# Layer trunk on one core: unread products between the halves of the input, rounding among square sums, a store from the scalar engine, and changed places for rotation, retention scores and routing

## The chip, the core and the metric

One program on one core of a Trainium2 chip. The time is device microseconds of one execution; several executions are taken and the median is compared. TensorE multiplies, VectorE and ScalarE work elementwise, GpSimd issues a few transfers, SyncE (SP) issues nearly all loads and the stores. A profile is one execution recorded by the hardware profiler.

## The reference

A decoder trunk of two layers on 256 tokens of width 1024, in float32:

```
layer 0: RMSNorm -> one projection (3744 columns) -> MLA (8 heads) beside retention (8 heads)
         -> output projection -> residual; RMSNorm -> SwiGLU (3584) -> residual
layer 1: RMSNorm -> one projection -> sliding-window attention (16 heads) beside stick-breaking (8)
         -> output projection -> residual; RMSNorm -> top-2-of-8 expert SwiGLU -> residual
final RMSNorm
```

Retention rotates its queries and keys, takes scores per head, multiplies them by a decay and by the values. The router takes `logits = h @ router` (8 columns), the two largest per token, and a softmax over these.

## The kernel before, in words

The program is one block with a written-out instruction list per engine; engines meet only through semaphores, and each engine's list is its order of work. Every weight is split: ScalarE rounds a piece of 128 x 1024 (a "unit") to a short float (`l0_hi`, `hi_unit`, L327), VectorE subtracts to get the rest (`l0_lo`, `lo_unit`, L331), and TensorE makes three products of the halves (`mm3`, L318 to L320). Four units are in flight; unit d + 3 is split while unit d is multiplied.

*Start.* SP loads a few constants, then x in two halves of 512 columns, with pieces of the first projection between them, then the other tables, `w_ukv`, `w_uq`, the router, and from unit 8 on pieces of the projection into four slots that have come free. TensorE multiplies a block of ones three times (`fill`, L2586), transposes the first half of x (`norm_pe`, L376), waits for the second, transposes it and goes on to the units 0 to 3 (the kv latents and the rotary key), 4 to 7 (the query latents), 8 to 15 (retention queries and keys) and so on (`l0_pe`, `project`). ScalarE takes the square sums of x (`sums_of_squares`, L340), VectorE their inverse root.

*Latents.* After unit 4 TensorE transposes the kv latents (`turn_latent`, L805), VectorE copies them with a gain (`latent_turned(3, 2, 0)`, L590) at d = 5 of its loop, ahead of the rest of unit 8, and TensorE multiplies them by `w_ukv` after units 6 and 7 (`keys_values`, L815). `rope_key` (L599 to L606) follows the rest of unit 9.

*Units 16 to 31.* TensorE alternates units with the eight heads of MLA: `scores`, `turn` (L862), `values`. VectorE does `minimum`, `normalised` (L649 to L652) and the rotation `rope_ret` of retention, whose second part stands whole at d = 17 and d = 18. Rotated blocks are transposed by `turn_ret` (L846) at the units in `RT_AT`, retention scores (`ret_scores`, L880, L881) are taken at the units in `RET_AT`, VectorE multiplies them by the decay (`decayed`).

*Routing.* After the last output product of layer 1, TensorE transposes the right half of h (L2183), multiplies by the router (L2175, 8 columns a product), makes unread products (L2190) while VectorE ranks the logits, gets places by products with a triangle and ones (L2200 to L2204), gathers the rows of the first expert by products with a pick matrix (`first_pe`, L2222, L2223), and transposes them (L2228) when VectorE has scaled them (L2351). ScalarE rounds (L2286), VectorE takes the rest (L2356), and the first expert's gate product begins (L318, `pre_hi`).

*End.* The four quarters of the output are stored by SP (L2528) in the order (0, 0), (0, 1), (1, 1), (1, 0), each when VectorE or ScalarE has scaled it.

The order on VectorE that the text speaks of:

```python
                if d == 5:
                    dve.wait_ge(tables_in, 16)
                    latent_turned(3, 2, 0)
...
                if d + 3 < L0_UNITS:
                    l0_lo(dve, d + 3)
```

Of the kernel before, what the change touches and what calls it, by code (L numbers as in the profile page):

```python
# [13 lines left out]
P = 128  # L14
# [65 lines left out]
def trunk(nc, x, consts, decay_t, ab_w_in, w_uq, w_ukv, ab_w_out, f_gate, f_up, f_down,  # L80
          cd_w_in, cd_w_out, router, m_gate, m_up, m_down, moe_gain, final_gain, out):
    with ExitStack() as ctx:
# [119 lines left out]

        PRE_HI_AT = (CONST_OFF + 4 * (CONST_AT["cos_m"] + 40), ARENA, ARENA + 4096, XN_AT)
# [21 lines left out]
        def sem(name):  # L225
# [53 lines left out]
                             "rstd_banked", "rstd_set"))  # L279
        first_banked, first_scaled, first_turned, first_hi, first_lo = (  # L280
# [86 lines left out]

        def norm_pe(pe, use, ks=range(KD)):
            for k in ks:
                if use == 0 and k % 4 == 0:  # L370
                    pe.wait_ge(x_in[k // 4], 16)
                    pe.wait_ge(consts_in, 16)
                if use and k % 4 == 0:
                    pe.wait_ge(h_done, 4 * use - 2 + k // 2)
                for tb in range(TB):
                    ins = nc.tensor.transpose(norm_bank(use, k)[:, tb * P:tb * P + P],  # L376
                                              h[:, tb, k * P:k * P + P], const("ident"))
                if k % 2:
                    ins.then_inc(xT_banked, 1)
# [72 lines left out]
        def l0_act(act):  # L452
# [86 lines left out]
            for d in range(L0_UNITS):  # L539
# [18 lines left out]
                if d + 3 < L0_UNITS and d != 1:  # L558
                    l0_hi(act, d + 3)
# [3 lines left out]
                if d == 1:  # L563
                    sums_of_squares(act, 0, False, (1,))
# [19 lines left out]
        def l0_dve(dve):  # L584
# [40 lines left out]
            def rope_ret(part, tb):  # L625
                dve.wait_ge(ab_evac, part + 3)
                w = slice(512 * part, 512 * part + 512)
                t = rope_t.rearrange("p (a h d) -> p a h d", a=2, d=64)
                rope(rqk_raw[:, tb, w].rearrange("p (h d) -> p h d", d=64),
                     bc(const("cos_r", 64 * tb, 64 * tb + 64), 8), bc(const("sin_r", 64 * tb, 64 * tb + 64), 8), 32,  # L630
                     t[:, 0], t[:, 1], rqk[:, tb, w].rearrange("p (h d) -> p h d", d=64)).then_inc(rqk_done, 1)
                dve.wait_ge(rqk_done, 2 * part + tb + 1)

# [73 lines left out]
            for d in range(L0_UNITS):  # L707
# [25 lines left out]
                if d in (17, 18):  # L733
                    rope_ret(1, d - 17)
# [20 lines left out]
        def l0_pe(pe):  # L755
# [150 lines left out]
            for d in range(L0_UNITS):  # L906
# [6 lines left out]
                if d == 4:  # L913
                    turn_latent(lat_kv, 2, (4,), 0)
# [1246 lines left out]
        lg, gt, eq, gt_eq, rank = (rt[:, a:b] for a, b in ((36, 52), (64, 192), (192, 320), (64, 320), (320, 336)))  # L2161
        sel = sel_r.bitcast(F32)
# [4 lines left out]
        def route_pe(pe):  # L2167
            def logits(ks):
                for k in ks:
                    if k < 6:  # L2170
                        pe.wait_ge(xT_hi_done, 3 * KD + k + 1)
                    else:
                        pe.wait_ge(x32_act, k - 5)
                    for tb in range(TB):
                        ins = nc.tensor.matmul(pb[4][:, tb * NE:tb * NE + NE], xT32[:, xT32_at[k], tb * P:tb * P + P],  # L2175
                                               router_sb[:, k, :], start=(k, tb) == (0, 0), stop=k == KD - 1,
                                               skip_group_check=True)
                return ins
# [13 lines left out]
            pe.wait_ge(router_in, 16)  # L2192
# [18 lines left out]
        def first_pe(pe):  # L2211

            pe.wait_ge(pick_done, 2)
            pe.wait_ge(rstd_done, 4)
            for tb in range(TB):
                ins = nc.tensor.matmul(pb[0][:, 0:1], pick[:, tb, :], rstd[:, tb:tb + 1], start=tb == 0, stop=tb == 1)
# [8 lines left out]
            for k in range(KD):  # L2225
                if k % 4 == 0:
                    pe.wait_ge(first_scaled, k // 4 + 1)
# [18 lines left out]
        def route_act(act):  # L2246
# [59 lines left out]
        def route_dve(dve):  # L2306
# [10 lines left out]
            rest(1, 0)  # L2317
            dve.wait_ge(logits_banked, 1)
            vs(nc.vector.tensor_copy(lg, pb[4][:, 0:16]))
# [13 lines left out]
            inverse_rms(dve, 3)  # L2333
            rest(1, 1)

# [7 lines left out]
            early_lo(dve, 0)  # L2343
# [4 lines left out]
            for r in range(2):  # L2348
                w = slice(512 * r, 512 * r + 512)
                dve.wait_ge(first_banked, r + 1)  # L2350
                nc.vector.scalar_tensor_tensor(out=first_rows[:, w], in0=pb[6 + r], scalar=place_rstd,  # L2351
                                               in1=g_moe_row[:, w], op0=ALU.mult, op1=ALU.mult).then_inc(first_scaled, 1)
            for j in range(4):
# [3 lines left out]
                                        first_bank(j), f32(hi_),  # L2357
                                        ALU.subtract).then_inc(first_lo, 1)
            vs(nc.vector.tensor_reduce(cmax, pb[5][:, 16:24], AX, ALU.max))
# [31 lines left out]
        def last_root(act, part):  # L2391
# [18 lines left out]
            nc.scalar.activation(xn[:, 1, 512:D], squares[:, 4, :], ACT.Copy, scale=rstd[:, 1:2]).then_inc(act_scaled, 1)  # L2410

# [23 lines left out]
        def _(sp):  # L2435
# [98 lines left out]
            sp.wait_ge(act_scaled, 1)  # L2534
            store(1, 1)
# [43 lines left out]
        def _(pe):  # L2579
# [5 lines left out]
            for n in (512, 512, P):  # L2585
                nc.tensor.matmul(pb[0][:, 0:n], fill[:, 0:P], fill[:, 0:n], start=True, stop=True)  # L2586
# [120 lines left out]
```

## Time and profile before

| | |
|---|---|
| runs | 1513.69, 1514.54, 1514.88 us; median 1514.54 |
| profiled execution | 1515.59 us |
| its span, first to last instruction | 1513.7 us |
| TensorE | busy 1500.1 us (99%), mean granted clock 0.994 |
| VectorE, ScalarE | busy 1264.2 us (84%), 1100.4 us (73%) |
| HBM | 447.37 MB read, 299 GB/s over the span |

In a row of a timeline stand the start in us, the busy time of the row, the engine, the line, the operation, what it writes and reads, its shape, how many instructions it merges (x8), and in brackets how long the engine had stood idle before and for whom. Ends of products are modelled. A product in float32 goes through TensorE as two instructions. The clock (PEclk) is the share of full speed that was granted to TensorE: 1.00 is 2.4 GHz, 0.50 is 1.2 GHz. The chain of waits follows the work that ended last back to the start.

### The profile page before, as it was taken

The page shows a single profiled execution, that of the slowest core. Times are in us where ns is not written, and L with a number is a line of the kernel's source. Part 1 is how long each engine was busy: PE and PEld are TensorE (multiplying, and loading weights), DVE is VectorE, ACT ScalarE, POOL GpSimd, SP SyncE. Part 2 cuts the span into 40 slices and gives each one's busy share as a digit, 9 for nine tenths or more (in the row PEclk, how much of TensorE's full clock was granted, in tenths as well). Part 3 has the DMA queues.
Part 4 walks back from the last instruction along what each step waited for, and adds up shares of the span by engine and source line. Part 5 has one row for each costly group of instructions (what it writes and reads, how often), then busy time and mean ns, then how long its engine had stood idle before and what let it go on. Part 6 is the DMA issues. An engine that isn't in the chain of part 4 may idle for free.

```text
span 1513.7 us, 22229 instructions
## 1 busy us (share of the span) xinstructions
PE 1500.1 (99%) x7294; PEld 1238.0 (82%) x7294; DVE 1264.2 (84%) x1559; ACT 1100.4 (73%) x1395; POOL 25.8 (2%) x25
## 2 busy tenths in 40 slices
PE   9999999999999999999999999999999999999997
PEld 7778888888877788888888888888888888888886
DVE  4577676666667779999999999999999999999997
ACT  6565555555567767888888888888788788788886
POOL 0000000000000000000000000000000000000000
PEclk9999999999999999999999999999999999999999
DMA  9533374565555459999999999999999999999970
GB/s 337 195 112 119 143 267 167 198 211 189 190 175 180 151 211 398 413 400 392 390 375 384 377 381 378 379 385 371 381 384 371 383 392 361 390 387 361 411 280 30
DMA packets 193512, 454.00 MB, mean 300 GB/s; under 512 B 8208, under 2 KB 12176, under 8 KB 193200
## 3 DMA queue, kind: packets, MB, share of 16 engines
q1 hardware_dynamic: 190848, 443.72, 78.7%
q0 software_dynamic: 2608, 9.57, 2.3%
q8 instruction: 30, 0.49, 0.1%
q14 instruction: 26, 0.21, 0.0%
HBM read 447.37 MB, written 5.90 MB: 299 GB/s over the span
## 4 chain that ended last, share of the span: by engine, by line
PE 98%; DVE 1%; DMA 0%; ACT 0%; issue 0%; SPq 0%; ACTq 0%
PE bank L318 27%; PE bank L320 26%; PE bank L319 26%; PE bank L1528 6%; PE bank L1531 3%; PE bank L2059 1%; PE bank L390 1%; PE bank L826 1%; PE bank L1503 0%; PE bank L1351 0%; PE bank L815 0%; PE bank L1342 0%; PE bank L376 0%; PE bank L1824 0%; DMA h<-x_dram 0%; PE bank L1381 0%
## 5 line engine op out<-in xcount | busy, mean ns | idle before, releaser
L331 DVE TENSOR_TENSOR w_lo<-ring_low,w_hi 128x1024 fp32r<-128x1024 f32 (+2 forms) x442 | 532.4, 1216 | 86.1 <-ACT w_hi L327 57.8
L327 ACT ACTIVATE w_hi<-ring_low 128x1024 fp32r<-128x1024 f32 (+2 forms) x442 | 465.5, 1055 | 131.8 <-PE bank L320 125.4
L331 DVE TENSOR_TENSOR w_lo<-ring,w_hi 128x1024 fp32r<-128x1024 f32 x330 | 397.2, 1222 | 35.2 <-ACT w_hi L327 12.4
L327 ACT ACTIVATE w_hi<-ring 128x1024 fp32r<-128x1024 f32 x328 | 346.4, 1061 | 81.0 <-PE bank L320 81.0
L318 PE MATMUL bank<-w_hi,xe_hi 128*128 128x512 f32 x888 | 350.3, 395 | 0.0
L320 PE MATMUL bank<-w_hi,xe_lo 128*128 128x512 f32 x888 | 346.1, 390 | 0.0
L319 PE MATMUL bank<-w_lo,xe_hi 128*128 128x512 f32 x888 | 345.5, 389 | 0.0
L320 PEld LDWEIGHTS bank<-w_hi,xe_lo 128*128 128x128 f32 x888 | 166.7, 188 | 35.5
L319 PEld LDWEIGHTS bank<-w_lo,xe_hi 128*128 128x128 f32 x888 | 166.9, 188 | 33.1
L318 PEld LDWEIGHTS bank<-w_hi,xe_hi 128*128 128x128 f32 x888 | 166.8, 188 | 32.9
L318 PE MATMUL bank<-w_hi,hT_hi 128*128 128x512 f32 x448 | 175.8, 392 | 0.0
L320 PE MATMUL bank<-w_hi,hT_lo 128*128 128x512 f32 x448 | 174.4, 389 | 0.0
L319 PE MATMUL bank<-w_lo,hT_hi 128*128 128x512 f32 x448 | 174.3, 389 | 0.0
L1528 PE MATMUL bank<-xT_both,w_hi 128*128 128x512 f32 x416 | 130.6, 395 | 0.0
L320 PEld LDWEIGHTS bank<-w_hi,hT_lo 128*128 128x128 f32 x448 | 84.1, 188 | 17.7
L318 PEld LDWEIGHTS bank<-w_hi,hT_hi 128*128 128x128 f32 x448 | 84.1, 188 | 17.2 <-DVE hT_lo L1962 0.2
L319 PEld LDWEIGHTS bank<-w_lo,hT_hi 128*128 128x128 f32 x448 | 84.1, 188 | 16.9
L1494 DVE TENSOR_TENSOR w_lo<-ring_low,w_hi 128x1024 fp32r<-128x1024 f32 x56 | 68.6, 1224 | 31.6 <-ACT w_hi L1486 30.1
L1531 PEld LDWEIGHTS bank<-xT_both,w_lo 128*128 128x128 f32 x416 | 78.1, 188 | 18.4
L318 PE MATMUL bank<-w_hi,xT_both 128*128 128x512 f32 (+3 forms) x224 | 89.0, 397 | 0.0
L1486 ACT ACTIVATE w_hi<-ring_low 128x1024 fp32r<-128x1024 f32 x56 | 59.1, 1056 | 35.5 <-PE bank L320 35.5
L320 PE MATMUL bank<-w_hi,xT_both 128*128 128x512 f32 (+3 forms) x224 | 83.9, 375 | 0.0
(340 smaller groups left out, 1674.4 us busy)
## 6 DMA issues: line engine op xcount, KB each, us to landing
ring<-m_gate_dram SPq DMA_DIRECT2D x72, 1024.0 KB, 6.1
ring_low<-m_down_dram SPq DMA_DIRECT2D x72, 1024.0 KB, 6.4
ring<-m_up_dram SPq DMA_DIRECT2D x56, 1024.0 KB, 6.9
ring_low<-m_up_dram SPq DMA_DIRECT2D x56, 1024.0 KB, 6.6
ring_low<-m_gate_dram SPq DMA_DIRECT2D x40, 1024.0 KB, 6.1
ring<-m_down_dram SPq DMA_DIRECT2D x40, 1024.0 KB, 6.5
ring_low<-f_gate_dram SPq DMA_DIRECT2D x14, 1024.0 KB, 5.2
ring_low<-f_up_dram SPq DMA_DIRECT2D x14, 1024.0 KB, 6.4
```

The lines of the kernel that those rows point to most:

```text
L318: nc.tensor.matmul(out_, a_hi, b_hi, start=first, stop=False, **kw)
L319: nc.tensor.matmul(out_, a_hi, b_lo, start=False, stop=False, **kw)
L320: return nc.tensor.matmul(out_, a_lo, b_hi, start=False, stop=last, **kw)
L327: nc.scalar.activation(w_hi[:, buf, 0:width], src, ACT.Copy).then_inc(hi_ready, 1)
L331: nc.vector.tensor_tensor(w_lo[:, buf, 0:width], src, f32(w_hi[:, buf, 0:width]), ALU.subtract).then_inc(split_ready, 1)
L390: ins = nc.tensor.matmul(pb[bank][half_rows(r), cols], v[r][0 if first else 1], a[r][:, src], start=first, stop=not first, skip_group_chec ...
L826: ins = nc.tensor.matmul(pb[((7, 4), (5, 6))[tb][nh]][:, 0:384], latT[:, k, tb * P:tb * P + P], ring[4 + nh][:, k * 384:k * 384 + 384], st ...
L1486: nc.scalar.activation(f_split(w_hi, u), f_block(kind, u), ACT.Copy).then_inc(hi_ready, 1)
L1494: nc.vector.tensor_tensor(f_split(w_lo, u), f_block(kind, u), f32(f_split(w_hi, u)), ALU.subtract).then_inc(split_ready, 1)
L1528: nc.tensor.matmul(pb[j], w_hi[:, j, k * P:k * P + P], xT_both[:, :, k, :], start=k == 0, stop=False, skip_group_check=True)
L1531: ins = nc.tensor.matmul(pb[j][:, 0:256], w_lo[:, j, k * P:k * P + P], xT_hi[:, k, :], start=False, stop=k == KD - 1, skip_group_check=True)
L2059: ins = nc.tensor.transpose(pb[6][:, j * PLACES:j * PLACES + PLACES], eh[c % 2][:, j * P:j * P + P], const("ident")[0:PLACES, 0:PLACES])
```

## The change

At the start two products of the block of ones, whose result nobody reads, stand between the two halves of x. ScalarE rounds unit 5 between the two square sums, and VectorE takes its rest before the inverse root. The kv latents are transposed after unit 5, and copied at d = 6 of VectorE's loop. The second rotation is cut in steps over d = 17 to 22, and its transposes move from units 20 and 22 to 22 and 23. Retention head 0 moves from unit 24 to unit 25, beside head 1, with a bank of its own. The router is copied, twice over, into a wide tile by ScalarE; the logits are taken transposed (72 rows, of which 8 are read, by 256 tokens), copied by VectorE and turned back by TensorE; the counts get a product of their own; the number of unread products changes from 9 and 5 to 4, 14 and 4; scale and rest of the first expert's rows alternate in quarters; several small works change place on VectorE. The third store is issued by ScalarE.

```diff
+        def unread_fill(*widths):
+            for n in widths:
+                nc.tensor.matmul(pb[0][:, 0:n], fill[:, 0:P], fill[:, 0:n], start=True, stop=True)
+
         def norm_pe(pe, use, ks=range(KD)):
             for k in ks:
+                if (use, k) == (0, 4):
+                    unread_fill(512, 512)
...
-        R_BANK = (7, 7, 7, 6, 7, 6, 7, 6)
-        RET_AT = {24: (0,), 25: (1,), 26: (2, 3), 27: (4, 5), 28: (6, 7)}
+        R_BANK = (4, 7, 7, 6, 7, 6, 7, 6)
+        RET_AT = {25: (0, 1), 26: (2, 3), 27: (4, 5), 28: (6, 7)}
...
-        RT_AT = {16: 0, 18: 1, 20: 2, 22: 3}
+        RT_AT = {16: 0, 18: 1, 22: 2, 23: 3}
...
-                if d + 3 < L0_UNITS and d != 1:
+                if d + 3 < L0_UNITS and d not in (1, 2):
                     l0_hi(act, d + 3)
                 if d == 0:
                     l0_hi(act, 4)
                     sums_of_squares(act, 0, False, (0,))
-                if d == 1:
+                    l0_hi(act, 5)
                     sums_of_squares(act, 0, False, (1,))
...
+            def rope_ret_part(tb, step):
...
-                if d == 5:
+                if d == 6:
                     dve.wait_ge(tables_in, 16)
                     latent_turned(3, 2, 0)
...
-                if d + 3 < L0_UNITS:
+                if d + 3 < L0_UNITS and d != 2:
                     l0_lo(dve, d + 3)
                 if d == 1:
+                    l0_lo(dve, 5)
                     inverse_rms(dve, 0)
...
-                if d in (17, 18):
-                    rope_ret(1, d - 17)
+                if 17 <= d <= 22:
+                    rope_ret_part((d - 17) // 3, (d - 17) % 3)
...
-                if i:
-                    pe.wait_ge(ret_decayed, {1: 2, 2: 4, 3: 2}.get(i, 2 * i - 2))
+                if i == 0:
+                    pe.wait_ge(nm_done, MLA_H)
+                if i > 1:
+                    pe.wait_ge(ret_decayed, {2: 4, 3: 2}.get(i, 2 * i - 2))
...
-                if d == 4:
+                if d == 5:
                     turn_latent(lat_kv, 2, (4,), 0)
...
-                    for tb in range(TB):
-                        ins = nc.tensor.matmul(pb[4][:, tb * NE:tb * NE + NE], xT32[:, xT32_at[k], tb * P:tb * P + P],
-                                               router_sb[:, k, :], start=(k, tb) == (0, 0), stop=k == KD - 1,
-                                               skip_group_check=True)
+                    ins = nc.tensor.matmul(pb[4][0:72, 0:256], router_wide[:, NE * k:NE * k + 72],
+                                           xT32[:, xT32_at[k], :], start=k == 0, stop=k == KD - 1)
...
-            pe.wait_ge(exact_set, 2)
-            unread_products(9)
+            pe.wait_ge(exact_set, 4)
+            unread_products(4)
+            pe.wait_ge(logits_copied, 1)
+            for tb in range(TB):
+                ins = nc.tensor.transpose(pb[4][:, 256 + tb * NE:256 + tb * NE + NE], lgT[0:NE, tb * P:tb * P + P],
+                                          const("ident")[0:NE, 0:NE])
+            ins.then_inc(logits_turned, 1)
+            unread_products(14)
...
-            for a in (8, 16):
-                nc.tensor.matmul(pb[5][:, a:a + 8], ones_r, sel_r[:, 0:NE], start=False, stop=False,
-                                 skip_group_check=True)
-            nc.tensor.matmul(pb[5][:, 16:24], ones_r, sel_r[:, NE:2 * NE], start=False, stop=True,
+            nc.tensor.matmul(pb[5][:, 8:16], ones_r, sel_r[:, 0:NE], start=False, stop=True,
                              skip_group_check=True).then_inc(pos_banked, 1)
-            unread_products(5)
+            for tb in range(TB):
+                ins = nc.tensor.matmul(pb[4][:, 272:280], ones_r, sel_r[:, tb * NE:tb * NE + NE], start=tb == 0,
+                                       stop=tb == 1, skip_group_check=True)
+            ins.then_inc(counted, 1)
+            unread_products(4)
...
+            act.wait_ge(t_done, SB_H)
+            act.wait_ge(router_in, 16)
+            for a, n in ((0, KD), (64, KD)):
+                nc.scalar.activation(router_wide[:, a:a + NE * n], router_sb[:, 0:n, :].rearrange("p k e -> p (k e)"),
+                                     ACT.Copy).then_inc(exact_set, 1)
...
             prepare_pick(dve, 0, 0)
-            early_lo(dve, 0)
+            rest(1, 1)
...
+            for j in range(4):
+                scaled(j)
+                if j:
+                    turned_rest(j - 1)
+            turned_rest(3)
+            early_lo(dve, 0)
+            dve.wait_ge(counted, 1)
...
+            act.wait_ge(act_scaled, 1)
+            act.dma_start(out[0, P:2 * P, 512:D], xn[:, 1, 512:D]).then_inc(out_done, 16)
...
-            sp.wait_ge(act_scaled, 1)
-            store(1, 1)
```

## Rows read from the trace of the kernel before

**Rows 1.** The page: span, and the chain that ended last, by engine.
```profile
span 1513.7 us, 22229 instructions
...
PE 98%; DVE 1%; DMA 0%; ACT 0%; issue 0%; SPq 0%; ACTq 0%
```

**Rows 2.** Timeline of TensorE, 0 to 33 us.
```profile
5.24 1.09 PE L376 MATMUL bank<-cst,h 128*128 128x128 f32 x8
8.28 1.92 PE L376 MATMUL bank<-cst,h 128*128 128x128 f32 x8 [1.95 <-DMA h<-x_dram]
...
23.91 3.60 PE L815 MATMUL bank<-ring_low,latT 128*128 128x512 f32 x8
...
32.45 0.79 PE L318 MATMUL bank<-w_hi,xT_both 128*128 128x512 f32 x1
```

**Rows 3.** Stretches at the start: busy us of PE, PEld, DVE, ACT, POOL; PEclk, DMA share, GB/s.
```profile
8.20:10.00 1.80, 1.72 (x9) 1.72 (x9) 1.75 (x4) 1.31 (x4) 0.00 (x0) 0.55 1.07 397
10.00:11.60 1.60, 1.60 (x8) 1.60 (x8) 1.34 (x3) 1.60 (x5) 0.00 (x0) 0.50 1.07 402
11.60:13.00 1.40, 1.40 (x12) 1.40 (x11) 1.40 (x4) 0.83 (x2) 0.00 (x0) 0.93 1.16 450
```

**Rows 4.** Timeline of VectorE, 19 to 31 us.
```profile
19.99 0.88 DVE L590 TENSOR_SCALAR latT<-bank,cst 128x256 f32<-128x256 f32 x2
...
27.57 2.36 DVE L331 TENSOR_TENSOR w_lo<-ring_low,w_hi 128x1024 fp32r<-128x1024 f32 x2 [6.64 <-ACT w_hi L327]
29.85 0.18 DVE L599 TENSOR_TENSOR rope_t<-lat_kv,cst 128x32 f32<-128x32 f32 x1
```

**Rows 5.** Timeline of ScalarE, 17 to 29 us.
```profile
17.39 0.89 ACT L460 ACTIVATE lat_kv<-bank,small 128x288 f32<-128x288 f32 x2
...
26.48 2.01 ACT L327 ACTIVATE w_hi<-ring_low 128x1024 fp32r<-128x1024 f32 x2 [6.34 <-DMA ring_low<-ab_w_in_dram]
```

**Rows 6.** Timeline of SP, 9 to 20 us: issues of loads.
```profile
13.93 6.66 SPq L408 DMA_DIRECT2D ring_low<-ab_w_in_dram  x2
```

**Rows 7.** The loads of the first projection (tensor ab_w_in_dram), 0 to 60 us.
```profile
DMA to landing us min/median/max: 4.9/7.6/12.5
```

**Rows 8.** Stretch of the routing, columns as in rows 3.
```profile
547.70:554.50 6.80, 6.40 (x24) 5.53 (x23) 4.23 (x11) 2.04 (x2) 0.00 (x0) 0.50 0.42 170
```

**Rows 9.** Timeline of TensorE, 78 to 97 us.
```profile
78.97 0.55 PE L862 MATMUL bank<-cst,p_sb 128*128 128x128 f32 x3 [0.55 <-DVE p_sb L652]
...
96.04 0.60 PE L846 MATMUL bank<-cst,rqk 128*128 128x128 f32 x4
```

**Rows 10.** Timeline of VectorE, 80 to 97 us.
```profile
80.22 0.69 DVE L606 TENSOR_TENSOR rqk<-rope_t 128x512 f32<-128x512 f32 x1
...
96.49 0.35 DVE L652 TENSOR_SCALAR p_sb<-p_sb,small 128x256 f32<-128x256 f32 x1
```

**Rows 11.** Timeline of TensorE, 105 to 115 us: scores of one head, then of two.
```profile
105.35 0.70 PE L880 MATMUL bank<-rT 64*128 64x256 f32 x2
...
113.79 0.71 PE L880 MATMUL bank<-rT 64*128 64x256 f32 x4
```

**Rows 12.** Timeline of TensorE, 544 to 557 us.
```profile
544.16 2.74 PE L2175 MATMUL bank<-router_sb,xT 128*128 128x8 f32 x24
...
551.48 0.77 PE L2222 MATMUL bank<-h_hi,pick_r 128*128 128x512 f32 x1
...
554.81 0.60 PE L2228 MATMUL bank<-cst,first_rows 128*128 128x128 f32 x4
...
556.23 0.47 PE L318 MATMUL bank<-pre_hi,xe_hi 128*128 128x512 f32 x1
```

**Rows 13.** Timeline of VectorE, 548 to 557 us.
```profile
548.46 0.17 DVE L2332 TENSOR_SCALAR sel_r<-rt 128x16 fp32r<-128x16 f32 x1
...
555.67 0.74 DVE L2356 TENSOR_TENSOR xe_lo<-bank,xe_hi 128x256 fp32r<-128x256 f32 x2
```

**Rows 14.** Timeline of SP, 1510.6 to 1511 us: the last two stores.
```profile
1510.19 1.22 SPq L2528 DMA_DIRECT2D out_dram<-xn  x2
```

More of the change, by code:

```diff
@@ L200, in trunk @@
         router_sb = place("router_sb", [P, KD, NE], at=SMALL + 768)
+        router_wide = place("router_wide", [P, 128], at=CONST_OFF + 4 * (CONST_AT["sb_neg"] + 256))
         PRE_HI_AT = (CONST_OFF + 4 * (CONST_AT["cos_m"] + 40), ARENA, ARENA + 4096, XN_AT)
@@ L279, in trunk @@
                              "rstd_banked", "rstd_set"))
+        logits_copied, logits_turned, counted = (sem(n) for n in ("logits_copied", "logits_turned", "counted"))
         first_banked, first_scaled, first_turned, first_hi, first_lo = (
@@ L632, in rope_ret @@
                 dve.wait_ge(rqk_done, 2 * part + tb + 1)
+            def rope_ret_part(tb, step):
+                if step == 0:
+                    dve.wait_ge(ab_evac, 4)
+                w = slice(512, 1024)
+                a, b = rope_t.rearrange("p (a h d) -> p a h d", a=2, d=64)[:, 0], \
+                    rope_t.rearrange("p (a h d) -> p a h d", a=2, d=64)[:, 1]
+                x_ = rqk_raw[:, tb, w].rearrange("p (h d) -> p h d", d=64)
+                cos, sin = (bc(const(name, 64 * tb, 64 * tb + 64), 8) for name in ("cos_r", "sin_r"))
+                if step == 0:
+                    vs(nc.vector.tensor_tensor(a, x_, cos, ALU.mult))
+                elif step == 1:
+                    vs(nc.vector.tensor_tensor(b[:, :, 0:32], x_[:, :, 32:64], sin[:, :, 0:32], ALU.mult))
+                    vs(nc.vector.tensor_tensor(b[:, :, 32:64], x_[:, :, 0:32], sin[:, :, 32:64], ALU.mult))
+                else:
+                    vs.settle()
+                    nc.vector.tensor_tensor(rqk[:, tb, w].rearrange("p (h d) -> p h d", d=64), a, b,
+                                            ALU.add).then_inc(rqk_done, 1)
+                    dve.wait_ge(rqk_done, 3 + tb)
             def minimum(i):
@@ L2161, in trunk @@
         lg, gt, eq, gt_eq, rank = (rt[:, a:b] for a, b in ((36, 52), (64, 192), (192, 320), (64, 320), (320, 336)))
+        lgT = rt[:, 768:1024]
         sel = sel_r.bitcast(F32)
@@ L2190, in unread_products @@
                     nc.tensor.matmul(pb[0][:, 0:256], ones_r, exact_r, start=True, stop=True)
-            pe.wait_ge(router_in, 16)
+            pe.wait_ge(exact_set, 2)
             turn_right(0)
@@ L2211, in first_pe @@
         def first_pe(pe):
-            pe.wait_ge(pick_done, 2)
             pe.wait_ge(rstd_done, 4)
             for tb in range(TB):
+                pe.wait_ge(pick_done, tb + 1)
                 ins = nc.tensor.matmul(pb[0][:, 0:1], pick[:, tb, :], rstd[:, tb:tb + 1], start=tb == 0, stop=tb == 1)
@@ L2225, in first_pe @@
             for k in range(KD):
-                if k % 4 == 0:
-                    pe.wait_ge(first_scaled, k // 4 + 1)
+                if k % 2 == 0:
+                    pe.wait_ge(first_scaled, k // 2 + 1)
                 ins = nc.tensor.transpose(first_bank(k // 2)[:, (k % 2) * P:(k % 2) * P + P],
@@ L2317, in route_dve @@
             rest(1, 0)
+            inverse_rms(dve, 3)
             dve.wait_ge(logits_banked, 1)
-            vs(nc.vector.tensor_copy(lg, pb[4][:, 0:16]))
+            nc.vector.tensor_copy(lgT[0:NE, :], pb[4][0:NE, 0:256]).then_inc(logits_copied, 1)
+            dve.wait_ge(logits_turned, 1)
+            vs(nc.vector.tensor_copy(lg, pb[4][:, 256:272]))
             vs.settle()
@@ L2332, in route_dve @@
             nc.vector.tensor_scalar(sel_r, rank, 2.0, None, ALU.is_lt).then_inc(sel_done, 1)
-            inverse_rms(dve, 3)
-            rest(1, 1)
             dve.wait_ge(sel_done, 1)
@@ L2347, in route_dve, with scaled, turned_rest @@
             dve.wait_ge(rstd_set, 1)
[L2348 to L2353, printed above, removed]
+            def scaled(j):
+                w, c0 = slice(256 * j, 256 * j + 256), 256 * (j % 2)
+                dve.wait_ge(first_banked, j // 2 + 1)
+                nc.vector.scalar_tensor_tensor(out=first_rows[:, w], in0=pb[6 + j // 2][:, c0:c0 + 256],
+                                               scalar=place_rstd, in1=g_moe_row[:, w], op0=ALU.mult,
+                                               op1=ALU.mult).then_inc(first_scaled, 1)
+            def turned_rest(j):
                 dve.wait_ge(first_hi, j + 1)
@@ L2584, in _ @@
             pe.wait_ge(fill_set, 1)
-            for n in (512, 512, P):
-                nc.tensor.matmul(pb[0][:, 0:n], fill[:, 0:P], fill[:, 0:n], start=True, stop=True)
+            unread_fill(512, 512, P)
             norm_pe(pe, 0)
```

5 lines of the change are left out of this document (2 added, 3 removed).

## The prediction, made blind

> **What bounds the kernel now.** I began with the page's chain of waits: TensorE holds 98% of it, and the span is 1513.7 us [rows 1]. So only two things count: time in which TensorE stands still or runs at half clock, and what a change adds to its queue. A microsecond saved or lost early is kept to the end, because the waits of TensorE that the profile shows are all short; the longest is 1.95 us at 8.28, for the second half of x [rows 2]. I then read the four places that the diff touches: the first 35 us on each engine, the units 16 to 28 of layer 0, the routing (542 to 562 us), and the stores.
>
> In the first 10 us the clock falls after that wait: 0.55 in 8.2 to 10.0, 0.50 (1.2 GHz) until 11.6, and near full only after that [rows 3]. The same eight transposes take 1.09 us ahead of the gap and 1.92 us behind it [rows 2]. Some 3.4 us at half clock cost 1.7 us of work.
>
> VectorE has something else to show. After the latent copy at 19.99 it idles 6.64 us, until 27.57, when it gets the rounded half of unit 8 from ScalarE [rows 4]; ScalarE itself waited 6.34 us for those weights and began at 26.48 [rows 5]. The load was issued at 13.93 [rows 6] and the slowest load of this tensor took 12.5 us to land [rows 7], which gives 26.4. DMA moves about 400 GB/s from 8 to 13 us [rows 3], so it is bandwidth, not the time of issue, that sets this. Before, nothing is lost by it: unit 8 is multiplied at 32.45 only [rows 2].
>
> **The change part by part.** *Start.* Two unread 512-column products fill the gap. The fill at the very start shows that they keep TensorE occupied; at full clock they take about 1.7 us (eight half-passes of 512 columns take 3.60 in the row at 23.91, four are 1.8 [rows 2]), which just fits in the 1.95. The clock then should not fall, and units 0 to 3 would end about 1.7 us sooner. Rounding unit 5 between the two square sums hands over its rest in time: square sums, evacuation and units 6 and 7 come some 0.3 to 0.8 us sooner on ScalarE, and turning the kv latents after unit 5 instead of 4 covers that. These cost nothing while units 4 to 6 (2.1 us each) hide them. TensorE would reach keys_values(0) at about 22.1 instead of 23.91.
>
> But keys_values(0) waits for latT_done, and the diff moves latent_turned on VectorE from d = 5 to d = 6. In that loop the rest of unit d + 3 stands behind it, so it stood ahead of the rest of unit 8 and now stands behind it. So it waits for the late weights: rounding 26.48 to 27.5, rest 27.57 to 28.75 (the row holds two in 2.36), two latent copies 0.88, done at 29.6 [rows 4, 5]. keys_values(0) starts at 29.63 instead of 23.91: 5.7 us later, after 7.5 us of idle, and the time won by the fill is swallowed whole. Queued behind the waiting VectorE instruction are the rest of unit 9, rope_key and, through TensorE, ScalarE's evacuation of keys and values. TensorE then restarts at half clock; nothing shows how long a stretch follows such a gap, so the bounds are 0 and the 3.4 us that the longest half-clock stretch (6.8 us [rows 8]) cost; I take 1.7, the price of the nearest row, the restart at 8.28. From 29.63 the old 8.54 us to unit 8 (23.91 to 32.45 [rows 2]) follow. **+7.4 us** (5.7 to 9.1).
>
> Can VectorE pass the wait? In the trace rope_key's first product of the key rows is ready when lat_kv is evacuated at 18.3 [rows 5], and it runs at 29.85, behind the two rests that stand ahead of it in the program, though VectorE was idle for 6.64 us [rows 4]. It does not pass. The Trainium skill ("TensorE: Matmul & The Clock Gate", section "Architectural detail: the array is 16× 32×32, not 1× 128×128") says that VectorE's queue is strict first-in first-out; by that the sum stays at +5.8, and were it otherwise it would be -3.4, so it takes chance from the third rival. The trace agrees, by the row at 29.85.
>
> *Rotation.* The second rotation is cut in three steps per block over d = 17 to 22. TensorE waited 0.55 us at 78.97 for a probability that VectorE delivered late behind the rotation [rows 9]; with the next unit's smaller slip I take -0.8 (0.5 to 1.0). But turn_ret(2) moves to d = 22 and needs the last step, which VectorE runs behind normalised(5) of the same d: that ends at 96.84, the step takes 0.69 as at 80.22 [rows 10], so 97.5, while TensorE was done with unit 22 at 96.04 [rows 9]. **+1.5** of new waiting. *Retention scores.* Heads 0 and 1 come as a pair in two banks. A single head's two products take 0.70 us, four of a pair 0.71 [rows 11]: a pair runs side by side, **-0.8** with its second, shorter group. The added wait on nm_done is long met by d = 25. Together -0.1 (-1.8 to +1).
>
> *Routing.* In 547.7 to 554.5 the clock is 0.50 [rows 8], after the 8-column logits products. The new logits, 72 rows by 256 columns, have no row. The nearest for their form is keys_values, 0.45 us per half-pass of 512 columns [rows 2], so 0.45 for a block's two half-passes of 256; the old form took 0.46 a block (24 products for six blocks in 2.74 [rows 12]). I take no difference; at half clock the six blocks would cost 2.7 more, which is the upper end. If this and the unread products hold the clock: the eight gather products, 551.48 to 554.81 [rows 12], take 1.8 instead of 3.3: -1.5. From the selection to the gather, 2.85 us before (548.63 [rows 13] to 551.48), half-clock products alternate with VectorE; after, two small products instead of four at full clock (0.4), VectorE's place and picks as before (0.7) and the root's products at full clock (0.4) leave an estimated 1.5: -1.4. Against it: a 256-column copy (0.44, as a latent copy [rows 4]) and two small transposes with the crossings between engines (0.3): +0.75. And the tail: before, 1.42 us lie between the last gather product and the expert's first (554.81 to 556.23). Now VectorE alternates scale and rest, and the rest of the first pair, which waits for TensorE and ScalarE, stands ahead of the scale of the third. Two transposes, rounding, rest, scale, rest, scale, two transposes: at 0.37 for a rest [rows 13], 0.44 for a scale and for a rounding, and 0.3 for each transposed pair, some 2.8: +1.4. **-0.8** (-1.5 to +2.7). early_lo(0), the counts and the gates, now later on VectorE, stay inside the 5.5 us of the expert's first 24 products; without that cover they would cost up to 1.2. The two ScalarE copies of the router fall into an idle stretch of 2.8 us.
>
> *Store.* SP issues the third and fourth store one behind the other, two issues in 1.22 us from 1510.19 on [rows 14]. With the third on ScalarE's queue the last can go at 1510.2: -0.7, a little over half of that (0 to 0.75: ScalarE's own issue has no row).
>
> **Sum:** +7.4 - 0.1 - 0.8 - 0.7 = +5.8. The profiled execution took 1515.59 (span 1513.7 and 1.9 around it) and would take 1521.4; it lies 1.05 above the median of 1514.54, so the median becomes **1520.3**.
>
> **Rivals.**
> - *The clock falls in the routing's tail too.* TensorE has only four pairs of transposes in 2.8 us there. For it: a gap of 1.95 us was enough at 8.28 [rows 2, 3]. The expert's first products would then lose 1.7 us: +7.5, 1522.0. The Trainium skill (same page, section "Part 4: PE-mode transpose") holds that transposes do not engage the full clock; by it this case is what happens. No row shows transposes alone. Chance 0.25.
> - *The weights come sooner.* At the median landing of 7.6 us [rows 7] unit 8 lands at 21.5, the latents are done at 24.7: +0.8 + 1.7 - 1.6 = +0.9, 1515.4, no change that a measurement tells. Against it: the same bytes stand ahead in the queue as before. Chance 0.08.
> - *Nothing is held (faster).* If unit 8's rest were ready by 21.2, that is, its weights by 18.9, latent_turned would end by 22.1, and the fill's 1.7 us would be kept: -1.8 - 0.1 - 0.8 - 0.7 = -3.4, 1511.1. This is also the case in which I misread the order. Against it: 26.48 [rows 5], 7.6 us too late. Chance 0.15.
> - *The fill does not keep the clock up:* changes nothing in the forecast, since TensorE waits anyway; in the case above it leaves -1.6.
>
> **How the numbers follow.** Forecast 0.52, the rivals as above. A measurement tells 0.2%, 3.0 us. Slower: forecast and first rival, 0.77; the same: the second and a fifth of the third, 0.11; faster: 0.12. The forecast's own bounds reach from +2 (no clock loss, best routing) to about +9; the range 1515.0 to 1524.4 holds the forecast and the first two rivals but for their ends: about 0.8.
>
> **What would show it.** In the profile after: VectorE's latent copies at about 28.7, behind the rest of unit 8; a TensorE wait of 7 us ahead of keys_values(0) at 29.6; a full clock from 8 to 22 us and half clock behind the wait; turn_ret(2) waiting 1.5 us for the rotation; one group of four in place of two single heads; no half clock in the gather, and a tail of 2.8 us; a last store 0.7 us sooner. If keys_values(0) starts at 22, the forecast is wrong and the third rival is right.

## The result, and the profile after

The changed kernel takes **1523.04 us** (median of six runs, 1522.53 to 1524.85) against 1514.41 of the kernel before in the same session: a ratio of 1.0057, 95% interval 1.0047 to 1.0067. It is slower, as forecast; 1520.3 was predicted, and the time lies inside the range 1515.0 to 1524.4.

| | before | after |
|---|---|---|
| median | 1514.41 us | 1523.04 us |
| profiled execution | 1515.59 us | 1522.53 us |
| its span | 1513.7 us | 1520.7 us |
| TensorE, share of the chain of waits | 98% | 92% |
| mean granted clock | 0.994 | 0.996 |

Between the profiles 7.0 us lie, between the medians 8.6: the profiled execution of before was one of its longer ones (1.2 us above its median), that of after one of its shorter ones (0.5 below). More on that with the fifth group of experiments.

The page of the kernel after, its span and its chain of waits (to be set against [rows 1]):

```profile
span 1520.7 us, 22230 instructions
...
PE 92%; DVE 0%; ACT 0%; issue 0%; ACTq 0%
```

The six points that TensorE lost are not the loss. The chain after is followed back only as far as 103.55 us, where that of before reaches 0.75, and the kernel with the latent copy put back (first group of experiments), which does not wait for the latents, has 93% and a chain that is followed back to 94.79. The timeline of TensorE shows where the time went (against [rows 2]):

```profile
6.55 1.88 PE L372 MATMUL bank<-fill 128*128 128x512 f32 x4
8.33 1.09 PE L384 MATMUL bank<-cst,h 128*128 128x128 f32 x8
...
29.30 5.61 PE L843 MATMUL bank<-ring_low,latT 128*128 128x512 f32 x8 [6.79 <-DVE latT L598]
...
39.86 0.79 PE L320 MATMUL bank<-w_hi,xT_both 128*128 128x512 f32 x1
```

The two unread products fill the gap and the second eight transposes take 1.09 us as the first do. Then keys_values (the products of the kv latents with `w_ukv`) waits 6.79 us for VectorE's copy of the latents, and unit 8 starts at 39.86 instead of 32.45: **+7.41** (predicted +7.4). ScalarE and VectorE in the same stretch (against [rows 4, 5]):

```profile
26.15 2.00 ACT L329 ACTIVATE w_hi<-ring_low 128x1024 fp32r<-128x1024 f32 x2 [6.70 <-DMA ring_low<-ab_w_in_dram]
```

```profile
27.24 1.23 DVE L333 TENSOR_TENSOR w_lo<-ring_low,w_hi 128x1024 fp32r<-128x1024 f32 x1 [7.92 <-ACT w_hi L329]
28.38 0.87 DVE L598 TENSOR_SCALAR latT<-bank,cst 128x256 f32<-128x256 f32 x2
...
30.36 0.18 DVE L607 TENSOR_TENSOR rope_t<-lat_kv,cst 128x32 f32<-128x32 f32 x1
```

The weights of unit 8 land at the same time as before (ScalarE begins at 26.15, before at 26.48). VectorE waits 7.92 us for them, takes the rest, and only then the copies that TensorE is waiting for; the key rows, evacuated at 17.6, again come after that. The stretches of TensorE show the price of the restart (columns: length, busy us and instructions of PE, PEclk, DMA share, GB/s):

```profile
26.00:28.00 2.00, 0.00 (x0) 0.59 1.05 409
28.00:30.00 2.00, 0.69 (x1) 0.50 1.05 410
30.00:32.00 2.00, 2.00 (x3) 0.50 1.05 409
32.00:34.00 2.00, 2.00 (x5) 0.71 1.05 386
```

The clock fell to 1.2 GHz in 26 to 28 us, while TensorE stood idle, and is back at 2.4 GHz from about 33 us on. From keys_values to unit 8 it takes 10.56 us where it took 8.54: 2.0 lost, 1.7 were taken for it.

What follows is small. Timeline of TensorE at the retention transposes and scores (against [rows 9, 11]):

```profile
103.59 0.66 PE L874 MATMUL bank<-cst,rqk 128*128 128x128 f32 x4 [1.30 <-DVE rqk L657]
...
117.11 0.71 PE L910 MATMUL bank<-rT 64*128 64x256 f32 x4
...
120.96 0.71 PE L910 MATMUL bank<-rT 64*128 64x256 f32 x4
```

The new wait is 1.30 us (1.5 predicted); heads 0 and 1 take 0.71 together. Heads 2 and 3 start at 113.79 before and at 120.96 after: the lag, by which the same work comes later than before, is 7.17 here. It was 7.41 at unit 8, so the rotation and the pair are worth -0.24 (predicted -0.1).

The routing on TensorE and on VectorE (against [rows 12, 13]):

```profile
551.29 2.75 PE L2205 MATMUL bank<-xT,router_wide 128*72 128x256 f32 x12
...
558.20 0.48 PE L2258 MATMUL bank<-h_hi,pick_r 128*128 128x512 f32 x1
...
560.13 0.76 PE L2264 MATMUL bank<-cst,first_rows 128*128 128x128 f32 x4
561.84 0.44 PE L2264 MATMUL bank<-cst,first_rows 128*128 128x128 f32 x2 [0.95 <-DVE first_rows L2392]
562.56 0.44 PE L2264 MATMUL bank<-cst,first_rows 128*128 128x128 f32 x2 [0.28 <-DVE first_rows L2392]
562.75 0.48 PE L320 MATMUL bank<-pre_hi,xe_hi 128*128 128x512 f32 x1
```

```profile
554.09 0.41 DVE L2361 COPY rt<-bank 8x256 f32<-8x256 f32 x1 [0.19 <-PE bank L2205]
...
556.40 0.17 DVE L2376 TENSOR_SCALAR sel_r<-rt 128x16 fp32r<-128x16 f32 x1
```

By these rows, from the end of the logits (554.04) on, where the figures of before come from [rows 12, 13]:

| step | before | after | difference | predicted |
|---|---|---|---|---|
| last six blocks of logits | 2.74 | 2.75 | 0 | 0 |
| logits to selection | 1.73 | 2.53 | +0.80 | +0.75 |
| selection to gather | 2.85 | 1.63 | -1.22 | -1.4 |
| gather | 3.33 | 1.93 | -1.40 | -1.5 |
| gather to the expert's first product | 1.42 | 2.62 | +1.20 | +1.4 |

The sum is -0.62 (predicted -0.8), and the lag at the expert's first product is 6.52. Two stretches of the tail, columns as above:

```profile
560.00:561.00 1.00, 0.89 (x6) 1.00 0.00 0
561.00:562.00 1.00, 0.17 (x1) 1.00 0.00 0
```

The clock stays at 2.4 GHz though TensorE is busy for only 0.17 of 561 to 562. The stores, on SP and on ScalarE's queue (against [rows 14]):

```profile
1515.32 2.04 SPq L2580 DMA_DIRECT2D out_dram<-xn  x3
```

```profile
1516.53 0.39 ACTq L2462 DMA_DIRECT2D out_dram<-xn  x1
```

SP is through with its last issue at 1517.36 instead of 1511.41: 5.95 later, with a lag of 6.84 ahead of it. So 0.9 was won there; but the span ends 3.3 us behind it, where it ended 2.3 behind it before, and nothing is left. (The lag of 6.84 is read from the rows on the expert in the part on the prediction.)

### The profile page after: what moved, and what is told of

The parts are those of the page before. It is cut to its first block, busy times and chain, and to the rows that moved or that the text cites. A ratio compares the mean times of both kernels' runs of the same rounds, so it can differ in the third digit from the quotient of the medians.

```text
span 1520.7 us, 22230 instructions
## 1 busy us (share of the span) xinstructions
PE 1500.9 (99%) x7292; PEld 1234.7 (81%) x7292; DVE 1264.6 (83%) x1562; ACT 1101.5 (72%) x1397; POOL 25.8 (2%) x25
## 4 chain that ended last, share of the span: by engine, by line
PE 92%; DVE 0%; ACT 0%; issue 0%; ACTq 0%
PE bank L320 25%; PE bank L322 25%; PE bank L321 25%; PE bank L1558 6%; PE bank L1561 3%; PE bank L2089 1%; PE bank L398 1%; PE bank L1533 0%; PE bank L1381 0%; PE bank L1372 0%; PE bank L1854 0%; PE bank L384 0%; PE bank L1411 0%; PE bank L1362 0%; PE bank L1535 0%; PE bank L2205 0%
## 5 line engine op out<-in xcount | busy, mean ns | idle before, releaser
L322 PEld LDWEIGHTS bank<-w_hi,hT_lo 128*128 128x128 f32 x448 | 84.1, 188 | 17.6
```

The costliest lines, as they stand in the source:

```text
L322: return nc.tensor.matmul(out_, a_lo, b_hi, start=False, stop=last, **kw)
```

## The experiments

All times are medians. There were three sessions, each with the kernel before beside it: it took 1514.32 us in the first (18 runs; groups 1 and 2, and the changed kernel without the fill of group 5), 1514.40 in the second (33; the three single kernels of group 3, and the copy back without the fill) and 1514.42 in the third (25; all three together, group 4, and the two products alone). Its profile was taken once more by itself.

**1. Is the place of the latent copy the whole loss?** One run undoes it in the changed kernel, one makes it alone in the kernel before.

```diff
-                if d == 6:
+                if d == 5:
                     dve.wait_ge(tables_in, 16)
                     latent_turned(3, 2, 0)
```

> The changed kernel with the latent copy on VectorE back at d = 5, ahead of the rest of unit 8; all else as changed. Theory (the place of the latent copy makes the loss): keys_values(0) starts at about 22 us instead of 29.3, no TensorE wait ahead of it, unit 8 some 1.7 us sooner than in the kernel before, and the sum of what is left (start -1.7, units 16 to 28 -0.3, routing -0.6, first expert +0.3, stores +0.2) gives about 1512.3, some 10.7 below the changed kernel. Rival (the cost lies in the work added in layer 0 and the routing): 1520 or more.

> The kernel before with one edit: the latent copy on VectorE at d = 6 instead of d = 5. Theory: TensorE waits from 23.9 to 29.5 us ahead of keys_values(0) and goes on at half clock, +5.6 for the wait and about +1.7 for the clock: 1521.7. Rival (the place alone is covered, and it takes the earlier TensorE of the whole change for a loss): 1514.4, as before.

Undone: **1513.85** (1513.63 to 1514.52; ratio 0.9995, 0.9986 to 1.0004), so all that made the change slower is gone, but there is no gain either; 1512.3 was expected. Alone: **1523.64** (ratio 1.0058, 1.0045 to 1.0072; 1521.7 expected). The one line costs 9.2 us by the first (1523.04 less 1513.85) and 9.3 by the second (less 1514.32). TensorE with the copy put back, and then with the copy moved alone:

```profile
22.54 3.60 PE L843 MATMUL bank<-ring_low,latT 128*128 128x512 f32 x8
...
31.08 0.79 PE L320 MATMUL bank<-w_hi,xT_both 128*128 128x512 f32 x1
```

```profile
8.90 1.09 PE L376 MATMUL bank<-cst,h 128*128 128x128 f32 x8 [1.73 <-DMA h<-x_dram]
...
29.65 5.71 PE L815 MATMUL bank<-ring_low,latT 128*128 128x512 f32 x8 [6.59 <-DVE latT L590]
...
40.30 0.79 PE L318 MATMUL bank<-w_hi,xT_both 128*128 128x512 f32 x1
```

With the copy at d = 5 nothing waits, though the transposes stand after unit 5 there too. Unit 8 moves from 31.08 to 39.86 by the one line: 8.78. In the second kernel there are no unread products and TensorE waits 1.73 us for x, but the transposes behind the wait take 1.09 us, at full clock, and not the 1.92 of [rows 2].

**2. Is it the weights that VectorE waits for?** The first piece of unit 8 is loaded ahead of w_uq and the router; the copy stays at d = 6.

```diff
+            sp.wait_ge(split_ready, 2)
+            ab_load(sp, 2, 0)
...
-            for c in range(2, 6):
+            sp.wait_ge(split_ready, 4)
+            ab_load(sp, 2, 1)
+            for c in range(3, 6):
```

> The changed kernel with one load moved: the first piece with unit 8 is issued ahead of the two query weights and the router (1.2 MB) instead of behind them. Theory (the rest of unit 8 is late because its weights land late, at the rate of the transfers): 1.2 MB at 400 GB/s are 3.0 us, so keys_values(0) starts at about 26.3 us and the time falls by 2 to 4, to about 1520. Rival (something else than the weights holds VectorE): keys_values(0) stays at 29.3, 1523.

**1519.40** (1517.45 to 1520.8; ratio 1.0027). ScalarE and TensorE of this kernel:

```profile
23.20 2.00 ACT L329 ACTIVATE w_hi<-ring_low 128x1024 fp32r<-128x1024 f32 x2 [3.83 <-DMA ring_low<-ab_w_in_dram]
```

```profile
26.36 6.68 PE L843 MATMUL bank<-ring_low,latT 128*128 128x512 f32 x8 [3.92 <-DVE latT L598]
```

ScalarE gets the weights 2.95 us sooner and TensorE goes on 2.94 sooner. The chain from load to rounding, rest, latent copy and keys_values holds link by link. The time does not follow it so closely: the profiled execution is the longest of the eight (1520.8), for the first products of keys_values take 6.68 where they took 5.61 after the longer wait, and two of the eight took 1517.5 and 1517.6. The granted clock is 0.996 in the longest, 0.997 in the five in between and 0.998 in these two, so by these the cost of the restart at half clock differs between executions of one kernel; only the longest has a profile.

**3. The small parts, with the copy at d = 5.** Each of three kernels takes back or shifts one more part of the change: the transposes of retention blocks 2 and 3 one unit later; the four scales ahead of the four rests; the third store on SP.

```diff
-        RT_AT = {16: 0, 18: 1, 22: 2, 23: 3}
+        RT_AT = {16: 0, 18: 1, 23: 2, 24: 3}
```

> The change with the latent copy back at d = 5, and the transposes of retention blocks 2 and 3 one unit later (units 23 and 24 for 22 and 23). Mine: the wait of 1.3 us ahead of the transposes of block 2 goes, since the last step of the rotation is done 1.5 us after unit 22 and unit 23 lasts longer; the scores of the second pair at unit 26 are far enough behind; 1512.6. Rival: the wait moves to the copies out of the bank or to the scores that read the turned blocks, and the time stays at 1513.85.

```diff
             for j in range(4):
                 scaled(j)
-                if j:
-                    turned_rest(j - 1)
-            turned_rest(3)
+            for j in range(4):
+                turned_rest(j)
```

> The change with the latent copy back at d = 5, and the four scales of the first expert's rows ahead of the four rests on VectorE, as they stand before the change. Mine: between the last gather product and the expert's first product 1.4 us lie in place of 2.6, 1512.7. Rival: the rests, now later, hold the expert's first product that reads them, and the 1.2 us come back as a wait inside the first unit; 1513.85.

```diff
-            act.dma_start(out[0, P:2 * P, 512:D], xn[:, 1, 512:D]).then_inc(out_done, 16)
...
+            sp.wait_ge(act_scaled, 1)
+            store(1, 1)
```

> The change with the latent copy back at d = 5 and the third store back on SP. Mine: the issue of the last store comes 0.7 us later and its landing takes some 0.9 us less, so 1513.8, within 0.3 of 1513.85. Rival, as in the prediction: the issue alone counts and the time is 1514.6.

The 1513.85 against which they are set is from the first session, and theirs is the second; the kernel before differs by 0.08 between the two.

| | median, range | against 1513.85 | expected |
|---|---|---|---|
| transposes later | 1512.23 (1512.0 to 1512.92) | -1.62 | -1.3 |
| scales first | 1512.67 (1512.18 to 1513.33) | -1.18 | -1.2 |
| store on SP | 1513.69 (1513.41 to 1514.2) | -0.16 | 0 |

Three signs of the forecast were tested here: the new wait and the longer tail are real losses, and the store from ScalarE brings nothing. The transposes of block 2 with one unit more, without a wait; and the tail with the scales first:

```profile
97.43 0.60 PE L874 MATMUL bank<-cst,rqk 128*128 128x128 f32 x4
```

```profile
550.98 1.57 PE L2264 MATMUL bank<-cst,first_rows 128*128 128x128 f32 x8
552.43 0.50 PE L320 MATMUL bank<-pre_hi,xe_hi 128*128 128x512 f32 x1
```

All eight transposes run in one piece, and 1.45 us lie between the gather and the expert where the other order takes 2.62. All three together:

> The change with four parts altered: the latent copy back at d = 5, the transposes of retention blocks 2 and 3 at units 23 and 24, the four scales ahead of the four rests, and the third store on SP. Mine: the two gains add, since they lie 450 us apart on TensorE and nothing behind either waits: 1513.85 - 1.6 - 1.2 = 1511.0 (1510.6 to 1511.4), 0.998 of the time before the change. Rival: the weights in the first expert's units are then what TensorE waits for, and one of the two gains is given back; 1512.2.

**1510.96** (1510.58 to 1511.42), ratio 0.9975 (0.9965 to 0.9985): faster than both kernels, and the two gains add up (1511.0 expected). All that TensorE still waits for 0.3 us or more (us in total, times, longest):

```profile
PE bank L372 <- DVE fill L2646: 1.5, 1, 1.5
PE bank L2128 <- DVE y_lo L2000: 0.3, 1, 0.3
```

**4. What holds the clock in the routing?** The gather runs at full speed after the change, but two edits could be why: the wide logits, or the unread products behind them. This kernel, with the copy at d = 5, has fewer of the latter.

```diff
-            unread_products(14)
+            unread_products(5)
```

> The change with the latent copy back at d = 5 and with 5 in place of 14 unread products behind the small transposes of the logits. Mine: TensorE then stands idle for some 1.2 us while VectorE ranks, as it did for 1.5 us behind the transposed rows, where the clock stayed at 1.00; what keeps the clock up in the routing is the 256-column form of the logits, so the gather still takes 1.9 us and the time is the same, 1513.85 within 0.4. Rival: the unread products keep it up; without nine of them the clock falls to 0.50, the gather takes 3.3 us and what follows is slower too: 1515.3 or more.

**1515.82**, and my expectation fell: the rival had 1515.3 or more. TensorE ahead of the places, and its stretches in the gather:

```profile
548.36 0.28 PE L2235 MATMUL bank<-sel_r,exact_r 128*128 128x16 f32 x1 [0.99 <-DVE sel_r L2376]
```

```profile
550.00:551.00 1.00, 1.00 (x4) 0.65 0.07 29
551.00:552.00 1.00, 1.00 (x4) 0.50 0.03 12
552.00:553.00 1.00, 1.00 (x4) 0.50 0.00 0
```

Nine unread products, 1.1 us of work that nobody reads (14 take 1.93, five 0.86), are worth 1.97 us at the median. Of the 2.0 between the two profiles 1.54 lie in the routing; TensorE was 0.47 later at the logits already. Three of the eleven executions took 1513.63 to 1513.94, with a granted clock of 0.998, the others 1515.55 to 1516.17, with 0.997, and none lay between: by these, whether the clock falls differs from one execution to the next, though only one of the long ones has a profile. The Trainium skill ("TensorE: Matmul & The Clock Gate", section "Part 1: The HAM clock gate (the "warmup" mystery)") says that the number of products that run at the low clock at the start of a kernel varies between runs of the same kernel. The eleven times show such a difference for a stretch in the middle. So the wide logits alone do not hold the clock. Whether the unread products would hold it with the old logits of 8 columns no run shows.

**5. What are the two unread products at the start worth?** They were taken out of the changed kernel, and out of the one with the copy at d = 5; put alone into the kernel before; and that kernel was profiled once more.

```diff
-                if (use, k) == (0, 4):
-                    unread_fill(512, 512)
```

> The changed kernel without the two unread products between the halves of x. Theory: their gain is swallowed by the wait, so the time stays at 1523.0 within 0.7, keys_values(0) again at about 29.3 us, with half clock from 8.3 to 11.8. Rival (the fill is worth its 1.7 us in the changed kernel too): 1524.7.

> The change with the latent copy back at d = 5 and without the two unread products between the halves of x. Mine: in the runs without them the clock stayed at 1.00 behind the wait for x, and the half clock of the profile of before was one execution's; then the fill is worth nothing at the median and this takes 1513.9 (1513.4 to 1514.4), as with the fill (1513.85). Rival, as in the prediction: the fill saves the 1.7 us of half clock in every execution, and without it the time is 1515.5. A third: the clock falls in some executions only, and the runs spread over 1.5 us where those with the fill spread over 0.9.

> The kernel before the change with the two unread products between the halves of x and nothing else of the change. Mine: ten of the last 33 executions of the kernel before lay at 1515.25 or above, as its profile with the half clock at 8.2 to 11.6 us did; if that fall is what makes them longer, none of this kernel's lies there, and the median stays near 1514.1. Rival, as in the prediction: every execution without the two products pays 1.7 us, and the median here is 1512.8.

> The kernel before the change once more, nothing altered, for a second profile of it. Mine: if this execution takes about 1514.2, the clock is at 1.00 from 8 to 13 us in spite of the wait for x, and unit 8 starts near 31 rather than 32.45; if it takes 1515.5 or more, the half clock of the first profile is there again. Rival: the half clock at the start is in every execution of this kernel, then it is there at 1514.2 as well, and the spread comes from another place.

Out of the changed kernel: **1523.11**, unchanged, as the prediction said for its case (the wait for the latents swallows what is won); the half clock that I expected behind its wait for x did not show. The wait was 0.80, and the transposes behind it ran at full speed:

```profile
8.19 1.09 PE L382 MATMUL bank<-cst,h 128*128 128x128 f32 x8 [0.80 <-DMA h<-x_dram]
```

Out of the one with the copy back: **1513.82** against 1513.85. Ten of the eleven took 1513.69 to 1514.06 and one 1515.37, with a granted clock of 0.997 where the ten have 0.998. So the third case of the expectation, a fall in some executions only, may be there in one of eleven; of that one there is no profile. The profiled one took 1513.88; TensorE in its stretches:

```profile
7.00:8.00 1.00, 0.38 (x2) 1.00 1.06 395
8.00:9.00 1.00, 0.48 (x4) 1.00 1.08 391
9.00:10.00 1.00, 1.00 (x11) 1.00 1.08 402
```

There is a gap (1.14 us), and the clock does not fall. The kernel before, profiled again, took 1516.06; and the half clock is there again, as expected for such a time; its second transposes, and two of its stretches:

```profile
8.44 1.71 PE L376 MATMUL bank<-cst,h 128*128 128x128 f32 x8 [1.99 <-DMA h<-x_dram]
```

```profile
9.00:10.00 1.00, 1.00 (x7) 0.50 1.08 404
10.00:11.00 1.00, 1.00 (x6) 0.50 1.06 399
```

So of five profiles without the two products two show the half clock of [rows 3], and both are long executions of the kernel before (1515.59 and 1516.06, where 60 of its 76 executions in the three sessions took less than 1515.35). The two products alone in the kernel before gave **1514.71** (ratio 1.0002, 0.9993 to 1.0011). My expectation fell here: the median is not near 1514.1, and one of the eleven, 1515.29, lies above the 1515.25 that none was to reach. The longest times of the kernel before, up to 1516.23, do not occur, but five of eleven lie between 1515.0 and 1515.3, and eleven are too few to say that the products keep anything away: 17 of the 76 executions without them took 1515.25 or more. (The ten of 33 in the expectation is a miscount; it is eight.) The rival's 1512.8 is excluded. TensorE in the profiled execution, which took 1514.06 (against [rows 2]):

```profile
22.43 3.60 PE L818 MATMUL bank<-ring_low,latT 128*128 128x512 f32 x8
```

Keys_values starts 1.48 sooner than in the first profile of the kernel before, and that lead is still 1.5 at the end of the span, so the half clock at the start is nearly all that parts these two executions. The spread of the kernel before goes with its clock: the 20 of its 76 executions with a granted clock of 0.994 took 1515.04 to 1516.23, and the 56 with 0.995 or 0.996 took 1513.48 to 1515.08. Where in the program the clock fell in them is open, and so is what an execution near 1514.2 looks like, as neither profile caught one.

## Why the prediction was right, and where it was not

**Right in mechanism and in size: the start.** The copy of the latents stood behind the rest of unit 8, the rest waited for weights that land at 26, and the fill's gain was swallowed. Its +7.4 was measured as +7.41. That it fits so closely is luck: keys_values began 0.33 sooner than predicted (29.30 for 29.63), and the restart at half clock cost 2.0 instead of 1.7, so two misses cancel. That VectorE does not pass a waiting instruction, on which it hung, is shown by the row at 30.36; the Trainium skill ("TensorE: Matmul & The Clock Gate", section "Architectural detail: the array is 16× 32×32, not 1× 128×128") says the same of its queue, and the trace agrees.

**Right: rotation, scores and routing.** Every step of the table above has its predicted sign, and each, like the rotation with the pair, is within 0.2 us of its forecast.

**Wrong: the first rival.** The clock did not fall in the tail of the routing; it was 1.00 throughout. The Trainium skill (same page, section "Part 4: PE-mode transpose") holds that transposes do not engage the full clock. Here only transposes ran from 560.13 to 562.75, with 1.2 us of waits between them, and the clock, already full, stayed full; a clock that rises on transposes alone no run here shows. (That no row shows transposes alone was not so either: the first eight of [rows 2] took 1.09 us at full clock, behind products.)

**Wrong: "stay inside the 5.5 us of the expert's first 24 products."** early_lo(0) and what now stands behind it are not wholly covered. From the gates' products to the next transposes of the expert part it took 11.39 us before and takes 11.70: 0.3 lost, where I had put nothing. TensorE before, and after:

```profile
561.78 0.51 PE L1841 MATMUL bank<-tok_gate,pick_r 128*128 128x9 f32 x4
...
573.17 0.49 PE L2059 MATMUL bank<-cst,eh 96*128 96x96 f32 x4
```

```profile
568.31 0.51 PE L1871 MATMUL bank<-tok_gate,pick_r 128*128 128x9 f32 x4
...
580.01 0.49 PE L2089 MATMUL bank<-cst,eh 96*128 96x96 f32 x4
```

The lag grows from 6.53 to 6.84. TensorE's weight loads in that stretch after, by what they wait for:

```profile
PEld bank L320 <- DVE w_lo L333: 0.5, 1, 0.5
```

A rest that VectorE takes behind the moved work comes late. With the four scales first the same way takes 11.55, so about half of the 0.3 goes with the order of scales and rests. No run moved early_lo alone, so which of the moved pieces makes the rest stays open.

**Wrong: the store's -0.7.** SP's last issue did come 0.9 sooner, but the landing behind it took 1.0 longer, and with the store back on SP the time was the same within 0.2. I had counted the issue and taken the landing as fixed. The other profiles show that the last issue does not set the end. From SP's first store to the end of the span 5.2 to 5.7 us pass in the six profiles with all four stores on SP, and 5.4 to 5.7 in the eight with the third on ScalarE; the sooner the last issue, the longer its landing (2.3 to 3.0 us in the six, 2.8 to 3.5 in the eight). What sets the end in its place stays open.

These add up: against a forecast of 1521.4 for the profiled execution 1522.53 was measured, of which the store makes 0.85 and the cover 0.3.

**Wrong: "it lies 1.05 above the median of 1514.54, so the median becomes 1520.3."** The excess of the profiled execution was subtracted as if it were a constant of the kernel. But the 1.7 us of half clock at the start, which the fill was to remove, are no loss of the median: the fill brought nothing out of the kernel with the copy back (1513.82 without it) and nothing into the kernel before (1514.71). Against the median the one line therefore costs 9.2 us, not 7.4 with a gain inside it. The forecast's difference was 5.8 (1520.3 less 1514.54), 8.6 was measured. Of the 2.9 between them 1.1 are the terms above and 1.2 are this step, by which the profile of before lies above its median. The last 0.5, by which the profile of after lies below its own, no run explains. That the half clock is missing from most executions of the kernel before is argued from these runs, and no profile of such an execution shows it.

## What to carry to other kernels

An instruction moved one loop step down an in-order queue is moved past everything between, waits included: ask for each of those what it waits for and when that arrives, and who waits for the moved one. Before pricing a stall or a low clock that a profile shows, compare the profiled execution with the spread of the runs: if it is a long one, its loss may be one that the median does not have. Alternating two kinds of work on one engine serves the consumer only if it needs both kinds in that order; where TensorE needs all the scaled rows, the rests between them are in its way.

## What was not expected of the hardware

With 14 unread products the clock stayed at 2.4 GHz through a following gather of 1.9 us; with five it fell to 1.2 GHz in the profiled execution and, by the times, in eight of eleven, and the median was 1.97 us longer. In the tail of the same routing two waits of 0.95 and 0.28 us with little but transposes around them did not lower it (560 to 563 us after the change). A wait of 1.73 us for x left the clock full in one kernel's profile, and waits of 1.95 and 1.99 us were followed by half clock in the other's two.
